# Seven products in the first stage's down part, and the attention mask added later

## The chip, the cores and the metric

One core of a Trainium2 chip runs the whole program. The metric is the device time of one execution in microseconds (us). The engines are TensorE (PE, matmuls into eight PSUM banks), VectorE (DVE), ScalarE (ACT), GpSimd (POOL) and SyncE (SP, which issues the weight loads). They run side by side and wait for each other through semaphores only.

## The reference

Input is x, 256 tokens of 1024 values in float32. A first block and two layers of a second block are computed, ten steps with a residual in all. The first step and the second, which this case is about, are:

```
f = (silu(n @ w_gate) * (n @ w_up)) @ w_down      # n = rms_norm(h) * pre gain; 1024 -> 2816 -> 1024
h = h + 0.5 * rms_norm(f) * post gain
q, k, v, xp, g_attn, g_pool = split(rms_norm(h) @ w_in)
s = q k^T / 8 over a neighbourhood + rpb bias; softmax; @ v    # 8 heads
m = (sigmoid(g_attn) * (y @ w_br_attn) + sigmoid(g_pool) * (pool(xp) @ w_br_pool)) @ w_out
h = h + rms_norm(m) * post gain
```

Then follow a second feed-forward step, a gated step on p, and the second block (feed-forward, gated linear attention, feed-forward, twice, the second time with retention). Everything is held to float32 accuracy.

## The kernel before

**Precision.** TensorE multiplies a reduced float32 format (fp32r). Each weight tile and each stationary block of tokens is therefore split in two: a high part, which ACT makes by a copy into fp32r (L1554 for weights), and a low part, the rest, which DVE makes by a subtraction (L2029). A product takes three runs of matmuls: high x high, token low x weight high (both want the high part), token high x weight low (wants the low part, so that comes last). A weight tile is 4 x 128 rows by 512 columns (1 MB, four "k"); the head tiles of the down weights have two k.

**Passes and products.** `pe_pass` multiplies one weight tile with one of two halves t of the tokens: 3 x 4 = 12 matmuls of 128x512, so a tile costs 24 (12 for a head tile). `pe_product` is one product of Strassen's scheme in Winograd's form: four tiles (two by two) with two token halves take seven products of 12 matmuls in place of eight passes of 12. It needs sums of token blocks (made and split once) and sums of weight tiles: t1 and t3 are a loaded tile to which POOL adds another by an accumulating DMA (`pool_sum`, L704), t2 and t4 are sums that DVE makes (L2033). The names of the products are b11, t1, t2, b22, t3, b21, t4.

**Stages.** The six feed-forward stages are f1, f2, a0, a1, b0, b1. Their gate and up part is an order of steps ("tile", "product", "turn"). A turn transposes 256 of the 2816 hidden values of both token halves (PE, L842), ACT copies it into `th` (L1559) and DVE makes `tl` (L2076). The last turns ("closing") lie in the down part. The down part has six row groups: group 0 (two k) and groups 1 to 5 (four k); group g needs the turned pieces 2g-1 and 2g. In f2, a0, a1, b0 and b1 the groups 2 and 3 are done as a unit of seven products (`pe_unit`, `dve_unit`, `DOWN_UNIT`); f1 does all groups in passes, group after group, with turns 8 and 7 behind groups 0 and 1. In all stages groups 4 and 5 close: first the four tiles for token half 0, then for token half 1, and ahead of the last pass PE transposes the next stage's x of token half 0 (`pe_turn_x`). The next stage starts with three passes and then transposes token half 1.

**The unit.** For it ACT copies four turned pieces once more, into `ua`, which lies in the buffer of the gains (L1700, ahead of the copy into `th`); DVE makes four sums `us`, ACT and DVE split them into `ush` and `usl`, which lie in the buffers `xh` and `xl` of the stage's x. In f2, whose result needs an rms norm before it goes into h, the products' shares are gathered in `xn` (`act_shared`, L1789; `take`, L2392), and at the edge DVE adds xn and the PSUM bank (L2116) before the arithmetic below. In a0 to b1 they are added to h directly.

**The edge** (`act_edge`, `dve_edge`; `to_mix` behind f1). For each token half ACT squares and sums the result (L1613), DVE multiplies it with a gain (L2122), adds up (L2124), ACT takes the root, DVE inverts it and updates h (L2133) and x (L2099). Between these the first tiles of the next stage are split: `early`, `mid`, `late` of the edge, (2, 1, 1) tiles for `to_mix`, (1, 2, 1) for most others. `src` is a PSUM bank.

**Weights.** SP loads tile after tile in the order of `load_key` and waits before each until its block is free. In f1 twelve blocks (of 14) hold whole, high and low parts; a planner (`give_blocks`, `give_slots`) gives each tile the block whose last user is oldest, a slot being a fixed pair of blocks. Blocks 12 and 13 hold the attention bias. ACT and DVE split in tile order, as far ahead as the blocks allow (`ahead`, `behind`, `act_high`, `dve_lows`).

**POOL's order.** Gains 1 and 2 by DMA, the mask, 16 parts of the bias with the four additions of f1 between them, then 16 additions of the mask to the bias (L722, each behind a given low of DVE), then gains 3 and 4 (each behind the last use of the gain before it), then three constants of the mixer, issued behind f1's last pass. The mixer's DVE adds the bias to the scores (L2479, one call for each head of two and each of 8 units), after a wait for the bias of its two heads.

Of the kernel before, what the change touches and what calls it, by code (L numbers as in the profile page):

```python
# [59 lines left out]
UNIT_ROWS = (2, 3)  # L60
# [18 lines left out]
UNIT_IN = ("f2", "a0", "a1", "b0", "b1")  # L79
# [82 lines left out]
def build(nc, A, out):  # L162
    with ExitStack() as ctx:
# [35 lines left out]
        xh = sb("xh", [P, 8, 256], F32R)  # L199
        xl = sb("xl", [P, 8, 256], F32R)  # L200
# [177 lines left out]
        def plan_ffn(name):  # L378
# [20 lines left out]
            if name not in UNIT_IN:  # L399
                plan_rows(name + "d", A[f"w_{name}_down"], A[f"w_{name}_down_head"])  # L400
                return
# [5 lines left out]

            p, q = UNIT_ROWS
            for step, *what in DOWN_UNIT:
# [55 lines left out]
        to_mix = edge(0, "mix", "rms", (1, 2), 4.0, "f1d", (2, 1, 1))  # L465
# [48 lines left out]
        def give_ffn(name, among, into_mixer=False):  # L514
# [5 lines left out]
            if name in UNIT_IN:  # L520
# [172 lines left out]
        def pool_sums(pool, name):  # L693
            for g in [group[name, n] for n in range(len(ORDER[name].pairs))] + (
                    [group[name + "d", 0]] if name in UNIT_IN else []):
# [10 lines left out]
        def pool_program(pool):  # L706
# [4 lines left out]
            pool_gain(pool, 1)  # L711
            pool_gain(pool, 2)
# [40 lines left out]
            pool.dma_start(pw[:, :, :], A["pool_w"][0].rearrange("g c d -> c g d")).then_inc(mix_in.mark("all"), 16)  # L753

# [68 lines left out]
        def unit_part(name, j):  # L823

            return [(m, 2 * j + 2 - 4 * g) for m, g in enumerate(UNIT_ROWS)
                    if name in UNIT_IN and 4 * g - 2 <= 2 * j < 4 * g + 2]

# [194 lines left out]
        def pe_ffn(pe, f):  # L1022
# [72 lines left out]
            if name in UNIT_IN:  # L1095
                pe_unit(pe, f, turn)
                dn = [None] * 8 + [spot[name + "d", g, n] for g in (4, 5) for n in range(2)]
            for g in range(0 if name in UNIT_IN else 4):
# [11 lines left out]
            for t in range(2):  # L1110
                for n in range(4):
# [5 lines left out]
                    if (t, n) == (1, 3) and f.nx == "out":  # L1117
                        if name in UNIT_IN:
# [5 lines left out]
        def pe_unit(pe, f, turn):  # L1124
# [10 lines left out]
            def tile(g, n):  # L1135
                for t in range(2):
                    if g == 0 and n == 1:
                        pe.wait_ge(vec.sem, vec.of("mult", name, order.plain[-2], t))
                    if n == 0 and t == 0:
                        pe.wait_ge(turn_lo.sem, turn_lo.of("t", name, order.last_turned(2 * g)))  # L1140
                    pe_pass(pe, spot[name + "d", g, n], T, groups[g][0], t, ACC[t][n], g == 0, False)

            def product(m):
                if m == "b11":
                    pe.wait_ge(turn_lo.sem, turn_lo.of("t", name, max(range(3, 7), key=order.turned.index)))
                    pe_product(pe, grp.b11, *block(0, grp.first), bank[0], True)
                elif m == "t1":
                    pe.wait_ge(fn.sem, fn.of("ush", name))
                    pe.wait_ge(vec.sem, vec.of("usl", name))
                    pe_product(pe, grp.t1, *sums(0), bank[1], True)  # L1150
                elif m == "t2":
                    if name == "f2":
# [3 lines left out]
                    pe_product(pe, grp.t2, *sums(1), bank[0], False)  # L1156
                elif m == "b22":
                    pe_product(pe, grp.b22, *sums(3), ACC[0][1], False)
                elif m == "t3":
                    pe.wait_ge(vec.sem, vec.of("ud", name, 0, 1, "t2"))  # L1160
                    pe_product(pe, grp.t3, *sums(2), bank[0], False)
                elif m == "b21":
                    pe_product(pe, grp.b21, *block(0, grp.second), ACC[0][0], False)
                else:
                    pe_product(pe, grp.t4, *block(1, grp.second), ACC[1][0], False)

            for step, *what in DOWN_UNIT:
# [431 lines left out]
        def act_post(act, e, t):  # L1599
# [5 lines left out]
            src = [half(xn[:, t, :], j) for j in range(2)] if e.nx == "pg" else edge_source(e, t)  # L1605
            for j in range(2):
                if e.kind == "ple":
                    act.wait_ge(vec.sem, vec.of("em", j, t))
                elif e.nx == "pg":
# [65 lines left out]
        def act_ffn(act, f, e):  # L1675
# [19 lines left out]
            def turn(j):  # L1695
                for m, k in unit_part(name, j):
                    act.wait_ge(turned.sem, turned.of("t", name, j))
                    if j == min(range(3, 7), key=order.turned.index):
# [62 lines left out]
            if name in UNIT_IN:  # L1761
                for step, *what in DOWN_UNIT:
                    if step == "tile":
                        act_high(act, ahead(spot[(name + "d", *what)], 1))
                    elif step == "product":
                        act_high(act, ahead(spot[name + "d", 0, what[0]], 1))
                        if name == "f2" and what[0] in ("b11", "t1", "t3"):
# [3 lines left out]
                    elif step == "blocks":  # L1771
                        act.wait_ge(vec.sem, vec.of("us", name, 3))
                        act.wait_ge(passed.sem, passed.of(gu[-1], 1))
                        act.activation(ush[:, :, :, :], us[:, :, :, :], ACT.Copy).then_inc(fn.mark("ush", name), 1)
# [7 lines left out]
        def act_shared(act, name, m):  # L1782
            act.wait_ge(passed.sem, passed.of(spot[name + "d", 0, m], 1))
            if m == "b11":
                act.wait_ge(vec.sem, vec.of("usl", name))
            if m == "t3":
                act.wait_ge(vec.sem, vec.of("ud", name, 1, 1, m))
            for t, n, b in {"b11": ((0, 0, 0),), "t1": ((0, 1, 1), (1, 1, 1)), "t3": ((1, 0, 0),)}[m]:
                act.activation(half(xn[:, t, :], n), bank[b][:, :], ACT.Copy).then_inc(fn.mark("ud", name, m), 1)  # L1789
# [500 lines left out]
        def dve_ffn(dve, f, e):  # L2290
# [76 lines left out]
            if name in UNIT_IN:  # L2367
# [8 lines left out]
        def dve_unit(dve, f, e, turn):  # L2376
# [11 lines left out]
            def take(t, n, after, m):  # L2388
# [3 lines left out]
                dve.tensor_tensor(x, x, bank[0][:, :], ALU.subtract).then_inc(vec.mark("ud", name, t, n, m), 1)  # L2392

            def products(m):
                if name == "f2":
# [4 lines left out]
                elif m == "b11":  # L2400
                    add(0, 0, bank[0], 1.0, m)
                elif m == "t1":
                    add(0, 1, bank[1], 1.0, m)
                    add(1, 1, bank[1], 1.0, m)
                elif m == "t2":
                    add(0, 1, bank[0], -1.0, m)
                elif m == "t3":
                    add(1, 1, bank[0], -1.0, m)
                    add(1, 0, bank[0], 1.0, m)
# [458 lines left out]
```

## Time and profile before

| | us |
|---|---|
| median of three runs | 1577.14 (1576.97 to 1578.09) |
| the profiled execution | 1576.5 |
| its span, first to last instruction | 1574.7 |
| PE busy in the span | 1564.3 |
| DVE busy | 1225.4 |
| ACT busy | 919.2 |
| POOL busy | 116.9 |

The granted TensorE clock was 0.999 of full speed. The busy time of PE includes matmuls that overlap; what one costs is read from the starts of those behind each other. In a timeline row the numbers are the start, the duration, the engine, the line, the operation, the written and read tiles, and how many instructions of the kind lie together; in brackets the idle time before them and what ended it.

### The profile page before, as it was taken

To read this page: it belongs to the slowest core of one execution; us is meant where nothing else is said; L and a number is where in the kernel's file an instruction comes from. 1 tells how busy PE (TensorE), PEld (TensorE's weight loads), DVE (VectorE), ACT (ScalarE), POOL (GpSimd) and SP (SyncE) were. 2 spreads that over 40 slices of the span, in tenths; PEclk is the share of its full clock that TensorE was granted. 3 is DMA by queue.
4 is the path that set the end of the run, shared out by engine and by line. 5 is a ranking of instruction groups with operands and counts; after the bars stand their busy time and mean duration, and the time that the engine had idled before them with its cause. 6 is when DMAs were issued, how large, how long until landed. Compare 5 with 4: busy or idle time off the path is not lost.

```text
span 1574.7 us, 18788 instructions
## 1 busy us (share of the span) xinstructions
PE 1564.3 (99%) x7587; PEld 1303.4 (83%) x7587; DVE 1225.4 (78%) x1168; ACT 919.2 (58%) x957; POOL 116.9 (7%) x138
## 2 busy tenths in 40 slices
PE   9999999999999999999999999999999999999998
PEld 6878897788888888888988888888888998888886
DVE  6888466677889779888658898878897657688887
ACT  7556456656675776654655575466654435455752
POOL 1115000000000000001010000000000131000000
PEclk9999999999999999999999999999999999999999
DMA  9896464467876687674648777868775544576773
GB/s 347 263 272 240 161 237 144 147 244 225 273 247 233 236 285 256 213 242 181 241 161 293 211 244 218 325 209 290 241 267 206 191 170 149 194 279 210 255 219 134
DMA packets 54484, 360.25 MB, mean 229 GB/s; under 512 B 6528, under 2 KB 6912, under 8 KB 13696
## 3 DMA queue, kind: packets, MB, share of 16 engines
q1 hardware_dynamic: 44864, 308.24, 52.0%
q0 software_dynamic: 9312, 50.70, 14.5%
q8 instruction: 60, 0.98, 0.3%
q14 instruction: 24, 0.20, 0.0%
q10 hardware_dynamic: 224, 0.14, 0.0%
HBM read 358.00 MB, written 1.05 MB: 228 GB/s over the span
## 4 chain that ended last, share of the span: by engine, by line
PE 98%; DVE 1%; DMA 0%; issue 0%; ACT 0%; SPq 0%; DVEq 0%; ACTq 0%
PE bank L892 22%; PE bank L905 22%; PE bank L896 19%; PE bank L959 7%; PE bank L954 7%; PE bank L956 7%; PE bank L842 3%; PE bank L909 3%; PE bank L988 2%; PE bank L990 2%; PE bank L991 2%; DVE split L2029 0%; DMA whole<-in_w_f_gate_up 0%; PE bank L1436 0%; PE bank L1226 0%; DVE whole L2033 0%
## 5 line engine op out<-in xcount | busy, mean ns | idle before, releaser
L2029 DVE TENSOR_TENSOR split<-whole,split 128x2048 fp32r<-128x2048 f32 (+2 forms) x346 | 741.8, 2168 | 113.5 <-ACT split L1554 112.6
L1554 ACT ACTIVATE split<-whole 128x2048 fp32r<-128x2048 f32 (+1 forms) x331 | 615.6, 1879 | 235.1 <-DVE whole L2033 59.8
L892 PE MATMUL bank<-split,xh 128*128 128x512 f32 x1020 | 279.6, 396 | 0.0
L905 PE MATMUL bank<-split,xh 128*128 128x512 f32 x1020 | 273.6, 390 | 0.0
L896 PE MATMUL bank<-split,xl 128*128 128x512 f32 x848 | 227.2, 390 | 0.0
L905 PEld LDWEIGHTS bank<-split,xh 128*128 128x128 f32 x1020 | 191.1, 188 | 40.8 <-DVE split L2029 0.6
L892 PEld LDWEIGHTS bank<-split,xh 128*128 128x128 f32 x1020 | 186.8, 188 | 39.4 <-issue 3.0
L896 PEld LDWEIGHTS bank<-split,xl 128*128 128x128 f32 x848 | 159.2, 188 | 34.2
L892 PE MATMUL bank<-split,th 128*128 128x512 f32 x364 | 101.0, 394 | 0.0
L896 PE MATMUL bank<-split,tl 128*128 128x512 f32 x364 | 99.4, 389 | 0.0
L905 PE MATMUL bank<-split,th 128*128 128x512 f32 x364 | 99.4, 389 | 0.0
L896 PEld LDWEIGHTS bank<-split,tl 128*128 128x128 f32 x364 | 68.3, 188 | 14.4
L905 PEld LDWEIGHTS bank<-split,th 128*128 128x128 f32 x364 | 68.3, 188 | 14.4
L892 PEld LDWEIGHTS bank<-split,th 128*128 128x128 f32 x364 | 67.1, 188 | 13.0
L2033 DVE TENSOR_TENSOR whole<-whole 128x2048 f32<-128x2048 f32 x34 | 77.6, 2284 | 0.0
L988 PE MATMUL bank<-xh,split 128*128 128x256 f32 x256 | 72.6, 284 | 0.0
L990 PE MATMUL bank<-xl,split 128*128 128x256 f32 x256 | 72.4, 283 | 0.0
L991 PE MATMUL bank<-xh,split 128*128 128x256 f32 x256 | 72.4, 283 | 0.0
L954 PE MATMUL bank<-split,xh 128*128 128x512 f32 x224 | 61.4, 396 | 0.6 <-DVE xn L2303 0.6
L2076 DVE TENSOR_TENSOR tl<-bank,th 128x512 fp32r<-128x512 f32 x66 | 45.4, 687 | 20.8 <-ACT th L1559 20.2
L956 PE MATMUL bank<-split,xl 128*128 128x512 f32 x224 | 60.0, 390 | 0.0
L959 PE MATMUL bank<-split,xh 128*128 128x512 f32 x224 | 60.0, 390 | 0.0
(335 smaller groups left out, 1998.5 us busy)
## 6 DMA issues: line engine op xcount, KB each, us to landing
whole<-in_w_a_gate_up SPq DMA_DIRECT2D x48, 1024.0 KB, 6.9
whole<-in_w_b_gate_up SPq DMA_DIRECT2D x48, 1024.0 KB, 6.9
whole<-in_w_f_gate_up SPq DMA_DIRECT2D x46, 1024.0 KB, 8.2
whole<-in_w_ret SPq DMA_DIRECT2D x24, 1024.0 KB, 4.8
whole<-in_w_a_down SPq DMA_DIRECT2D x22, 1024.0 KB, 6.8
whole<-in_w_b_down SPq DMA_DIRECT2D x22, 1024.0 KB, 6.8
whole<-in_w_f_down SPq DMA_DIRECT2D x21, 1024.0 KB, 4.9
whole<-in_w_mix SPq DMA_DIRECT2D x16, 1024.0 KB, 4.9
```

What stands on the lines that cost most here:

```text
L892: pe.matmul(o[:, :], tokens(0, k), whi[:, k, :], start=start and k == 0, stop=False, skip_group_check=True)
L896: pe.matmul(o[:, :], tokens(1, k), whi[:, k, :], start=False, stop=False, skip_group_check=True)
L905: ins = pe.matmul(o[:, :], tokens(0, k), wlo[:, k, :], start=False, stop=end, skip_group_check=True)
L954: pe.matmul(o[:, :], xh_of(k), whi[:, k, :], start=start and k == 0, stop=False, skip_group_check=True)
L956: pe.matmul(o[:, :], xl_of(k), whi[:, k, :], start=False, stop=False, skip_group_check=True)
L959: ins = pe.matmul(o[:, :], xh_of(k), wlo[:, k, :], start=False, stop=k == 3, skip_group_check=True)
L988: pe.matmul(o, whi[:, k, cols], xh[:, k0 + k, :], start=start and k == 0 and c % 2 == 0, stop=False, skip_group_check=True)
L990: pe.matmul(o, whi[:, k, cols], xl[:, k0 + k, :], start=False, stop=False, skip_group_check=True)
L991: ins = pe.matmul(o, wlo[:, k, cols], xh[:, k0 + k, :], start=False, stop=end, skip_group_check=True)
L1554: act.activation(split[s][:, 0:n], whole[r][:, 0:n], ACT.Copy).then_inc(hi.mark(i), 1)
L2029: dve.tensor_tensor(split[r][:, c0:c1], whole[r][:, c0:c1], split[s][:, c0:c1].bitcast(F32), ALU.subtract).then_inc(lo.mark(*what), 1)
L2033: dve.tensor_tensor(whole[load_to[i]][:, :], whole[load_to[a]][:, :], whole[load_to[b]][:, :], ALU.add).then_inc(vec.mark("sum", i), 1)
```

## The change

f1 gets a unit too, of the row groups 1 and 2 (`UNIT["f1"]`), with its own orders for PE and ACT (`F1_UNIT`) and DVE (`F1_UNIT_DVE`): tiles of groups 0 and 3 and the turns 8 and 7 lie between the products. Turns 1 to 4 make the second copy into `ua`; since `ua` lies in the gains' buffer, gains 1 and 2 are loaded only after the sums (`pool_gain(pool, g, "f1")`), behind the unit's two additions by DMA. The sums lie in `usx`, on the memory of `xl`, since `xn` still holds products of gate and up; they wait for the last pass over x. The products' banks are 6 and 7. Like f2, f1 gathers the shares in `xn`, so its edge adds xn and the bank first. The edge's tiles are (1, 2, 1), and only the last four down tiles get fixed slots. The 16 mask additions move behind gains 3 and 4 and the mixer's constants, in an order by pairs of heads, and no longer wait for DVE's lows.

```diff
+F1_UNIT = (
+    ("tile", 0, 0), ("tile", 0, 1), ("blocks",), ("turn", 8), ("tile", 3, 0), ("turn", 7),
+    ("product", "b11"), ("tile", 3, 1), ("product", "t1"), ("product", "b22"),
+    ("product", "t2"), ("product", "b21"), ("product", "t3"), ("product", "t4"))
+F1_UNIT_DVE = (
+    ("sums",), ("lows", 0, "b11"), ("turn", 8), ("blocks",), ("turn", 7), ("lows", 3, 1), ("lows", 0, "t1"),
+    ("lows", 0, "b22"), ("lows", 0, "t2"), ("lows", 0, "b21"),
+    ("add", "t2"), ("lows", 0, "t3"), ("lows", 0, "t4"), ("add", "t3"))
...
+UNIT = {"f1": Unit((1, 2), F1_UNIT, F1_UNIT_DVE),
+        **{name: Unit((2, 3), DOWN_UNIT, DOWN_UNIT_DVE) for name in ("f2", "a0", "a1", "b0", "b1")}}
+GATHERED = {"f1": "mix", "f2": "pg"}
...
+        with ExitStack() as first:
+            usx = sb("usx", [P, 4, 4, P], F32, first)
         xl = sb("xl", [P, 8, 256], F32R)
...
-        to_mix = edge(0, "mix", "rms", (1, 2), 4.0, "f1d", (2, 1, 1))
+        to_mix = edge(0, "mix", "rms", (1, 2), 4.0, "f1d", (1, 2, 1))
...
-                    give_slots(end - 4, end, [[5], [6], range(5), range(5)])
+                    closing = [[s] for s in slots if s >= 5]
+                    give_slots(end - 4, end, closing + [range(5)] * (4 - len(closing)))
...
-            pool_gain(pool, 1)
-            pool_gain(pool, 2)
...
-            for t in range(2):
-                pool.wait_ge(bias_in[t].sem, bias_in[t].of(7))
-                for hd in range(8):
-                    pool.wait_ge(lo.sem, lo.of(at["f1d"][t] + hd // 2))
-                    pool_mask(t, hd)
+            pool_sum(pool, "t1", group["f1d", 0].t1)
+            pool_sum(pool, "t3", group["f1d", 0].t3)
+            for g in (1, 2):
+                pool_gain(pool, g, "f1")
             for g in (3, 4):
                 pool_gain(pool, g)
...
             pool.dma_start(pw[:, :, :], A["pool_w"][0].rearrange("g c d -> c g d")).then_inc(mix_in.mark("all"), 16)
+            for t in range(2):
+                pool.wait_ge(bias_in[t].sem, bias_in[t].of(7))
+            for n in range(16):
+                pool_mask(n // 2 % 2, 2 * (n // 4) + n % 2)
...
+                    if g == 0 and n == 0 and name == "f1":
+                        pe.wait_ge(vec.sem, vec.of("mult", name, order.plain[-1], t))
...
-            src = [half(xn[:, t, :], j) for j in range(2)] if e.nx == "pg" else edge_source(e, t)
+            src = [half(xn[:, t, :], j) for j in range(2)] if e.nx in GATHERED.values() else edge_source(e, t)
...
+                        i = ahead(spot[(name + "d", *what)], 1)
+                        act_high(act, min(i, group[name + "d", 0].b11) if what[0] == 0 else i)
...
-            if e.nx == "pg":
-                dve.wait_ge(fn.sem, fn.of("ud", "f2", "t3"))
+            if e.nx in GATHERED.values():
+                dve.wait_ge(fn.sem, fn.of("ud", "f1" if e.nx == "mix" else "f2", "t3"))
...
             def sums():
-                dve.wait_ge(turned.sem, turned.of("t", name, ORDER[name].turned[-2]))
-                dve.wait_ge(fn.sem, fn.of("ua", name, max(range(3, 7), key=ORDER[name].turned.index)))
+                us = unit_sums(name)
+                if name == "f1":
+                    dve.wait_ge(passed.sem, passed.of(at[name + "gu"][-1], 1))
+                else:
+                    dve.wait_ge(turned.sem, turned.of("t", name, ORDER[name].turned[-2]))
+                dve.wait_ge(fn.sem, fn.of("ua", name, unit_turned(name)[-1]))
```

## Rows read from the trace of the kernel before

**Rows 1.** The page's first part: busy us (share of the span), instructions.

```profile
PE 1564.3 (99%) x7587; PEld 1303.4 (83%) x7587; DVE 1225.4 (78%) x1168; ACT 919.2 (58%) x957; POOL 116.9 (7%) x138
```

**Rows 2.** Waits of PE: engine line, releaser: us in all, times, longest.

```profile
PE bank L959 <- DVE split L2029: 0.7, 1, 0.7
PE bank L954 <- DVE xn L2303: 0.6, 1, 0.6
```

**Rows 3.** Timeline of PE, down part: start us, us, engine, line.

```profile
130.32 0.61 PE L892 MATMUL bank<-split,th 128*128 128x512 f32 x2
...
163.93 1.07 PE L892 MATMUL bank<-split,th 128*128 128x512 f32 x4
164.83 1.07 PE L896 MATMUL bank<-split,tl 128*128 128x512 f32 x4
```

**Rows 4.** Timeline of ACT, second stage, a turn of the unit.

```profile
444.58 0.60 ACT L1700 ACTIVATE gain<-bank 128x512 f32<-128x512 f32 x1
445.06 0.60 ACT L1559 ACTIVATE th<-bank 128x512 fp32r<-128x512 f32 x1
```

**Rows 5.** Timelines of ACT, DVE and PE behind turn 3.

```profile
60.56 0.60 ACT L1559 ACTIVATE th<-bank 128x512 fp32r<-128x512 f32 x1 [3.53 <-PE bank L842]
...
61.19 0.69 DVE L2076 TENSOR_TENSOR tl<-bank,th 128x512 fp32r<-128x512 f32 x1 [1.83 <-ACT th L1559]
...
70.61 2.28 DVE L2029 TENSOR_TENSOR split<-whole,split 128x2048 fp32r<-128x2048 f32 x1
...
73.59 4.48 DVE L2029 TENSOR_TENSOR split<-whole,split 128x2048 fp32r<-128x2048 f32 x2
...
72.18 1.07 PE L956 MATMUL bank<-split,sl 128*128 128x512 f32 x4
...
75.93 1.20 PE L905 MATMUL bank<-split,xh 128*128 128x512 f32 x4
```

**Rows 6.** Timeline of DVE, down part: a low beside masks.

```profile
142.83 2.84 DVE L2029 TENSOR_TENSOR split<-whole,split 128x2048 fp32r<-128x2048 f32 x1 [0.59 <-ACT split L1554]
```

**Rows 7.** Weight tiles, 130 to 200 us, and timeline of ACT, second stage.

```profile
DMA to landing us min/median/max: 4.7/4.9/7.0
...
502.30 1.92 ACT L1554 ACTIVATE split<-whole 128x2048 fp32r<-128x2048 f32 x1 [0.59 <-DMA whole<-in_w_f_down]
504.87 1.92 ACT L1554 ACTIVATE split<-whole 128x2048 fp32r<-128x2048 f32 x1 [0.65 <-DMA whole<-in_w_f_down]
```

**Rows 8.** Timelines of ACT, DVE and PE, edge into the mixer.

```profile
192.25 1.92 ACT L1554 ACTIVATE split<-whole 128x2048 fp32r<-128x2048 f32 x1 [2.12 <-DMA whole<-in_w_mix]
...
194.20 2.29 DVE L2029 TENSOR_TENSOR split<-whole,split 128x2048 fp32r<-128x2048 f32 x1 [3.24 <-ACT split L1554]
196.41 1.28 DVE L2122 TENSOR_TENSOR xn<-bank,gain 128x512 f32<-128x512 f32 x2
197.61 0.15 DVE L2124 TENSOR_TENSOR st<-st 128x1 f32<-128x1 f32 x1
...
199.30 1.07 PE L905 MATMUL bank<-split,xh 128*128 128x512 f32 x4
200.39 1.26 PE L842 MATMUL bank<-ident,xn 128*128 128x128 f32 x8
```

**Rows 9.** Timelines of DVE and ACT, closing arithmetic of the second stage.

```profile
514.23 0.69 DVE L2116 TENSOR_TENSOR xn<-xn,bank 128x512 f32<-128x512 f32 x1 [1.23 <-PE bank L905]
...
514.96 0.63 ACT L1613 ACTIVATE junk<-xn 128x512 bf16<-128x512 f32 x1 [1.20 <-DVE xn L2116]
...
515.71 0.69 DVE L2122 TENSOR_TENSOR xn<-xn,gain 128x512 f32<-128x512 f32 x1 [0.19 <-ACT junk L1613]
```

**Rows 10.** Mask additions (min/median/max ns), timelines of POOL and DVE.

```profile
L722 POOL TENSOR_TENSOR bias<-bias,mask x16: 731/745/2834, 128.2 to 148.3; 128x256 f32<-128x256 f32 x16
...
202.84 0.77 POOL L753 DMA_DIRECT2D pw<-in_pool_w  x1
...
243.30 0.74 DVE L2479 TENSOR_TENSOR pr<-bank,bias 128x256 f32<-128x256 f32 x2
```

More of the change, by code:

```diff
@@ L406, in rows @@
                 return full[g - 1, n] if g else head[n]
-            p, q = UNIT_ROWS
-            for step, *what in DOWN_UNIT:
+            p, q = UNIT[name].rows
+            for step, *what in UNIT[name].steps:
                 if step == "tile":
@@ L823, in unit_part, with unit_turned, unit_bank, unit_sums @@
         def unit_part(name, j):
-            return [(m, 2 * j + 2 - 4 * g) for m, g in enumerate(UNIT_ROWS)
-                    if name in UNIT_IN and 4 * g - 2 <= 2 * j < 4 * g + 2]
+            return [(m, 2 * j + 2 - 4 * g) for m, g in enumerate(UNIT[name].rows) if 4 * g - 2 <= 2 * j < 4 * g + 2]
+        def unit_turned(name):
+            p, q = UNIT[name].rows
+            return sorted([j for g in (p, q) for j in (2 * g - 1, 2 * g)], key=ORDER[name].turned.index)
+        def unit_bank(name, n):
+            return bank[6 + n] if name == "f1" else bank[n]
+        def unit_sums(name):
+            return (usx if name == "f1" else us)[:, :, :, :]
         def turn_bank(pe, key, by):
@@ L1155, in product @@
                         pe.wait_ge(vec.sem, vec.of("ud", name, 0, 0, "b11"))
-                    pe_product(pe, grp.t2, *sums(1), bank[0], False)
+                    pe_product(pe, grp.t2, *sums(1), unit_bank(name, 0), False)
                 elif m == "b22":
-                    pe_product(pe, grp.b22, *sums(3), ACC[0][1], False)
+                    pe_product(pe, grp.b22, *sums(3), acc[0][1], False)
                 elif m == "t3":
                     pe.wait_ge(vec.sem, vec.of("ud", name, 0, 1, "t2"))
-                    pe_product(pe, grp.t3, *sums(2), bank[0], False)
+                    pe_product(pe, grp.t3, *sums(2), unit_bank(name, 0), False)
                 elif m == "b21":
-                    pe_product(pe, grp.b21, *block(0, grp.second), ACC[0][0], False)
+                    pe_product(pe, grp.b21, *block(0, grp.second), acc[0][0], False)
                 else:
-                    pe_product(pe, grp.t4, *block(1, grp.second), ACC[1][0], False)
-            for step, *what in DOWN_UNIT:
+                    pe_product(pe, grp.t4, *block(1, grp.second), acc[1][0], False)
+            for step, *what in UNIT[name].steps:
                 if step == "tile":
@@ L1697, in turn @@
                     act.wait_ge(turned.sem, turned.of("t", name, j))
-                    if j == min(range(3, 7), key=order.turned.index):
+                    if j == unit_turned(name)[0] and name != "f1":
                         act.wait_ge(vec.sem, vec.of(*gain_end[e.gains[0] - 1]))
@@ L1773, in act_ffn @@
                         act.wait_ge(passed.sem, passed.of(gu[-1], 1))
-                        act.activation(ush[:, :, :, :], us[:, :, :, :], ACT.Copy).then_inc(fn.mark("ush", name), 1)
+                        act.activation(ush[:, :, :, :], unit_sums(name), ACT.Copy).then_inc(fn.mark("ush", name), 1)
             else:
@@ L1788, in act_shared @@
             for t, n, b in {"b11": ((0, 0, 0),), "t1": ((0, 1, 1), (1, 1, 1)), "t3": ((1, 0, 0),)}[m]:
-                act.activation(half(xn[:, t, :], n), bank[b][:, :], ACT.Copy).then_inc(fn.mark("ud", name, m), 1)
+                act.activation(half(xn[:, t, :], n), unit_bank(name, b)[:, :], ACT.Copy).then_inc(
+                    fn.mark("ud", name, m), 1)
         def act_mixer(act):
@@ L2425, in dve_unit @@
             added = {}
-            for step, *what in DOWN_UNIT_DVE:
+            for step, *what in UNIT[name].dve:
                 if step == "sums":
```

60 lines of the change are left out of this document (30 added, 30 removed).

## The prediction

> **What bounds the kernel now.** I read the page's busy times first, then TensorE's waits, then the timelines of PE, DVE, ACT and POOL from 28 to 262 us (first feed-forward stage and head of the mixer), and last the second feed-forward stage, which already has such a unit. TensorE is busy 1564.3 of 1574.7 us [rows 1]: it is the bound, and time is won by taking matmuls out or lost by making it wait. Two of its four listed waits are in the first stage, both short and both ended by DVE: 0.65 us for a product of gate and up, 0.74 us for the low half of a weight tile [rows 2]. So DVE is the engine to fear there.
>
> All instants below are on the clock of the trace of before; the unit lies at 130.3 to 166.7 us, and what follows it moves 2.72 us earlier if nothing waits.
>
> **The matmuls.** Row groups 1 and 2 of the down weights took eight passes of 12 matmuls, 96; the seven products take 84. Groups 0, 3, 4 and 5 keep theirs, and the two transpositions stay. Four matmuls start every 0.90 to 0.91 us (163.93, 164.83) [rows 3], 0.227 us each, not the 0.39 a row shows for one, since they overlap. Gain: 12 x 0.227 = 2.72 us, all on the path. It is also all that the change can give by its own terms.
>
> **The four copies into ua (ScalarE, gate and up phase).** Turns 1 to 4 now copy the transposed block a second time, ahead of the copy into th. In the second stage the second copy starts 0.48 us after the first (444.58, 445.06) [rows 4]. At turns 1, 2 and 4 the delay falls into idle time of ACT or DVE (turn 2: DVE then idles 1.8 us; turn 4: DVE is in a row of lows until 82.4). Turn 3 is different. th starts at 60.56, DVE's tl at 61.19, right behind it, and from there DVE works without a gap to 82 us. The low half of t2 ran 70.61 to 72.89, and PE wants it at 72.18 + 0.91 = 73.09; the low of tile (9,0) starts at 73.59, ends at 75.87, and PE takes it at 75.93, 0.06 later: it is already just in time [rows 5]. With 0.48 more, t2's low is there at 73.43 (0.34 lost) and the next at 76.41 for 75.93. Loss 0.48 us. Bounds: 0 (if DVE starts its row earlier), and 4 x 0.48 = 1.9.
>
> **DVE and ACT inside the unit.** Added: four sums, one split of them (ush, usl), two weight sums, three more weight splits on each engine, some copies and takes. A low or a weight sum costs DVE 2.20 us (two in 4.48) [rows 5]. By the new order and its planner's rule DVE reaches the four sums at about 132 (gate/up ends at 130.3; [rows 3]), earlier than the last multiplication's 134.8 of before since tile (3,0) is left for the unit. From 132.2: sums 2.6, (3,0) 2.2, b11 2.2, tl(8) 0.7, usl 2.2 (142.1); tl(7) waits for its turn to 143.5; (3,1) 2.2, sum 2.2, t1 2.2 (150.1), b22 2.2, sum 2.2, t2 2.2 (156.7), b21 158.9, take, t3 162.0, t4 164.2. PE wants the lows two thirds into each product: t1 152.1, b22 154.8, t2 157.5, b21 160.2, t3 162.9, t4 165.7. The least slack is 0.8 us, so 0 taken. Bounds: 0, and 1.7 us (if DVE reaches the sums at 134.8 as its old work did: 2.6 less 0.9). The 16 mask additions leave this stretch, where they stretched lows (one to 2.84 from 2.28) [rows 6]; that helps DVE and is worth nothing, as PE did not wait.
>
> **The closing weights.** I followed the planner's oldest-block rule. The four closing tiles A to D need slots that the products just used, and slot 6 is closed in this stage. A and B are freed by t1, b22 and b21 and come early; C's block is freed only by t3, at 163.9, and D, and the mixer's tiles 0 and 1, queue behind it on SP. A load lands 4.9 us after its issue (median; 4.7 to 7.0), and loads in a row come 2.5 us apart (502.30, 504.87) [rows 7]. C: 169.0, high 171.0, low 173.3; PE needs 172.1 and 173.9. D: 171.5, low 175.8, needed 176.6. Slack 0.6: 0 taken. Upper bound with the 7.0 us landing: low at 175.4, 1.5 us lost. Tile 0 of the mixer then comes at 174.0, later than now, its low ends at 178.3, the two additions at 179.6, and the rest of token half 0's arithmetic takes as long as now, some 5 us; PE wants its result at 185.7, so about 1 us of slack is left there.
>
> **The edge into the mixer.** This is the second loss. For token half 1 everything hangs on the mixer's tile 2, whose block is freed by a closing pass: it arrives at 192.2, ACT splits it, DVE makes its low (194.20 to 196.4), then the products with the gain start (196.41), their sum of squares at 197.61, and PE's transposition of the normed x, which could have begun at 199.30 + 0.91 = 200.21 starts at 200.39: this chain has no slack at all now [rows 8]. The change puts the addition of xn and the bank ahead of it: y0 and y1 (0.60 each, behind one another), and the square can only start behind y. In the second stage y1 starts at 514.23, its square at 514.96, the gain product at 515.71 [rows 9]: 1.48 from y1's start to the second gain product. So with the low ended at 196.41: y1 at 197.01, second gain product 198.5, the small sum at 199.16 in place of 197.61. Loss 1.55 us. Both the load and PE move by the same 2.72, so the difference stands. Bounds: 0, and 3.0 (four extra instructions of 0.69 and a handoff, all in line).
> The order (1,2,1) of the edge's loads takes one low from before token half 0's arithmetic to behind it; DVE has 1 to 2 us there: nothing.
>
> **Gains and masks.** Gains 1 and 2 are now loaded behind the unit's sums and t3's addition, at about 142, more than 30 us before the closing arithmetic wants the first: nothing. POOL's queue then has gains 3 and 4, three constants, and the masks. The last constant is issued at 202.84; a mask takes 0.745 us (median) and 2.834 at the longest; the first logit, at 243.30, needs four masks [rows 10]. Even at 2.834 each the first four are done by 214.2 and all sixteen by 248.2, when no more than the third logit is due, which needs eight: nothing. The other side of it is DVE: the mask's extra 2.1 us and the 0.56 us that a low grew to 2.84 show that the two hold each other up, and four or five lows of the mixer's head will now lie beside masks. That is the third rival. The Trainium skill (SBUF — State Buffer, "Who interferes with whom") has it as a rule: a DVE instruction with two SBUF inputs and a GpSimd one that reads SBUF exclude each other for a whole instruction; the trace agrees in kind, and by the rule a low could wait for a whole mask, 0.745 us, rather than 0.56.
>
> **Sum.** -2.72 + 0.48 + 1.55 = -0.69 us. The profiled execution took 1576.5 (span 1574.7 and 1.8 around it), 0.6 under the median 1577.14 of the three timed runs: 1576.5 - 0.7 = 1575.8, and against the median 1577.1 - 0.7 = **1576.4**.
>
> **Rivals.**
> 1. Everything is hidden: 1577.1 - 2.7 = 1574.4. For: the same unit in the second stage runs without a PE wait, and its y additions too. Against: there the closing chain does not hang on a load freed by the last passes. Between it and mine (one of the two losses only): 1574.9 or 1576.0.
> 2. The other side: C comes late. Its load hangs on t3's pass, 8.2 us before its first use and 10.0 before PE wants its low, where landing, high and low take 4.9 + 1.9 + 2.3 = 9.1, with handoffs 9.4. From a landing of over 5.5 us PE waits one for one; over 6.2 the kernel is slower than before. At 7.0: -0.69 + 1.5 = +0.8, so 1577.9; if D and the unit's lows slip as well (+1.7), 1579.6. For: the 7.0 occurs in this stretch [rows 7], and no other stage has a closing slot less. Against: 4.9 is usual.
> 3. The masks lengthen five lows of DVE in the mixer's head by 0.56 each, and PE waits for all of it: +2.8, 1579.2. Against: DVE idles between these lows, waiting for ACT, and they end well ahead of PE.
> That the products would not replace the passes I rule out by the code.
>
> **Chances.** Mine 0.50, rival 1 (with its halves) 0.25, rival 2 0.17, rival 3 0.03, something unseen 0.05. A difference under 0.2% (3.2 us) can't be told from none here. Even rival 1 stays inside, so faster 0.05 (an unseen wait that goes), slower 0.08 (the deep end of rival 2, rival 3), same 0.87. Range: from 1574.2, just under rival 1, to 1578.8, inside rival 2.
>
> **What would show it.** Right: 12 fewer 128x512 matmuls on th/tl and blocks (252 in the stage, 84 of them products); near 73 us a PE wait on DVE grown by 0.3 and the tile behind by 0.1; the unit free of waits; PE waiting some 1.7 us for the transposition near 198 to 199 us, with DVE's addition, ACT's square and the gain product in line before it. Wrong: a PE wait on ACT or DVE for a weight tile in the closing passes (rival 2), no wait at the transposition (rival 1), the logits waiting for POOL. If mixer tile 2 arrives earlier relative to PE, my largest loss falls.

## The result and the profile after

The changed kernel takes 1589.83 us (median of 6 runs, 1589.11 to 1591.33), the one before beside it 1577.17 (6 runs): ratio 1.0081, 95% interval 1.0069 to 1.0093. It is 12.7 us slower where I forecast 0.7 faster, far outside my range. The profiled execution took 1589.11 us, its span is 1587.1 at a mean granted clock of 0.996.

The page's busy row and TensorE's waits of the changed kernel (line, releaser: us in all, times, longest):

```profile
PE 1565.6 (99%) x7575; PEld 1303.0 (82%) x7575; DVE 1253.8 (79%) x1184; ACT 930.5 (59%) x969; POOL 109.4 (7%) x140
...
PE bank L917 <- ACT xh L1586: 11.0, 1, 11.0
PE bank L984 <- DVE split L2060: 0.9, 2, 0.8
PE bank L979 <- DVE xn L2334: 0.6, 1, 0.6
```

The 12 matmuls are gone (7587 to 7575 against [rows 1]), the waits of [rows 2] are about as they were, and one wait is new and nearly as large as the whole loss. Its releaser reads "ACT xh", the copy of the mixer's normed x; but ACT had been idle itself, so the chain has to be followed one step further. The timeline of DVE, PE, POOL and ACT around it (start, duration, engine, line; in brackets the idle time before it and its releaser):

```profile
198.90 1.26 PE L867 MATMUL bank<-ident,xn 128*128 128x128 f32 x8 [0.34 <-DVE xn L2130]
...
199.36 2.36 DVE L2060 TENSOR_TENSOR split<-whole,split 128x1024 fp32r<-128x1024 f32 x2
...
201.31 0.77 POOL L763 DMA_DIRECT2D pw<-in_pool_w  x1
...
201.63 11.41 DVE L2135 TENSOR_TENSOR st<-st 128x1 f32<-128x1 f32 x1
201.84 1.07 PE L930 MATMUL bank<-split,xh 128*128 128x512 f32 x4
202.09 10.93 POOL L733 TENSOR_TENSOR bias<-bias,mask 128x256 f32<-128x256 f32 x16
213.08 0.29 ACT L1617 ACTIVATE st<-st,eps 128x1 f32<-128x1 f32 x1 [13.46 <-DVE st L2135]
213.28 1.06 ACT L1586 ACTIVATE xh<-bank 128x512 fp32r<-128x512 f32 x2
213.41 0.16 DVE L2138 RECIPROCAL st<-st 128x1 f32<-128x1 f32 x1 [0.36 <-ACT st L1617]
...
213.91 2.08 PE L917 MATMUL bank<-split,xh 128*128 128x512 f32 x4 [11.00 <-ACT xh L1586]
...
215.78 1.91 PE L930 MATMUL bank<-split,xh 128*128 128x512 f32 x4
...
218.81 1.07 PE L917 MATMUL bank<-split,xh 128*128 128x512 f32 x4
```

Read from the bottom: PE waits for ACT's copy, ACT for its root, the root for DVE's small sum of squares, one element per partition. That sum is recorded with 11.41 us, and in just that time GpSimd runs all sixteen mask additions without a break. By the recorded starts the sum even comes first, 0.46 us ahead of the first mask. In the kernel before, the same sum and the low ahead of it:

```profile
200.85 2.36 DVE L2029 TENSOR_TENSOR split<-whole,split 128x1024 fp32r<-128x1024 f32 x2
203.13 0.16 DVE L2104 TENSOR_TENSOR st<-st 128x1 f32<-128x1 f32 x1
```

The second part of the loss stands in the windows of the changed kernel (the stretch, its length, then the busy us of PE, PE's weight loads, DVE, ACT and POOL, then the granted clock, DMA share, GB/s):

```profile
199.00:202.00 3.00, 3.00 (x17) 2.47 (x18) 3.00 (x4) 0.62 (x3) 2.26 (x4) 1.00 0.39 132
202.00:213.90 11.90, 0.91 (x5) 0.41 (x3) 11.54 (x6) 0.82 (x3) 11.01 (x17) 0.76 0.38 129
213.90:218.80 4.90, 4.89 (x12) 3.85 (x13) 2.75 (x4) 3.40 (x4) 0.00 (x0) 0.55 0.00 0
218.80:222.00 3.20, 3.20 (x16) 2.64 (x15) 0.82 (x1) 0.27 (x1) 0.00 (x0) 1.00 0.58 177
```

After 11 us of idling the granted clock is 0.55, near the lower level of 1.2 GHz, and 12 matmuls take 4.90 us where twelve at full clock take 2.72: 2.18 us more. Then it is back at 1.00.

The sum from the first stage to the second feed-forward stage: 0.45 (the gate and up phase starts that much later in this execution) + 0.48 (turn 3) - 2.72 (matmuls) + 0.32 (transposition) + 11.16 (from the last matmul's end at 202.75 to 213.91) + 2.18 (clock) = 11.87. The two traces are 11.82 apart there (479.00 against 467.18 for the same matmul). The spans differ by 12.4; the other 0.6 come later, most of it (0.36) behind the end of b0, where e12 below takes it up.

### The profile page after: what moved, and what is told of

Its sections match the earlier page's. It is cut to its first block, busy times and chain, and to the rows that moved or that the text cites. A ratio compares the mean times of both kernels' runs of the same rounds, so it can differ in the third digit from the quotient of the medians.

```text
span 1587.1 us, 18811 instructions
## 1 busy us (share of the span) xinstructions
PE 1565.6 (99%) x7575; PEld 1303.0 (82%) x7575; DVE 1253.8 (79%) x1184; ACT 930.5 (59%) x969; POOL 109.4 (7%) x140
## 4 chain that ended last, share of the span: by engine, by line
PE 93%; DVE 3%; DMA 1%; ACT 1%; issue 1%; SPq 0%; DVEq 0%; ACTq 0%
PE bank L917 21%; PE bank L930 20%; PE bank L921 17%; PE bank L984 7%; PE bank L979 7%; PE bank L981 7%; PE bank L867 3%; PE bank L934 3%; PE bank L1013 2%; PE bank L1015 2%; PE bank L1016 2%; DVE split L2060 1%; DVE st L2135 1%; DMA whole<-in_w_mix 1%; DVE whole L2064 1%
## 5 line engine op out<-in xcount | busy, mean ns | idle before, releaser
L917 PE MATMUL bank<-split,xh 128*128 128x512 f32 x1020 | 280.7, 397 | 11.0 <-ACT xh L1586 11.0
L930 PE MATMUL bank<-split,xh 128*128 128x512 f32 x1020 | 274.4, 391 | 0.0
L917 PEld LDWEIGHTS bank<-split,xh 128*128 128x128 f32 x1020 | 187.3, 189 | 51.0 <-ACT xh L1586 11.4
L921 PE MATMUL bank<-split,xl 128*128 128x512 f32 x848 | 227.2, 390 | 0.0
L917 PE MATMUL bank<-split,th 128*128 128x512 f32 x332 | 92.3, 394 | 0.0
L930 PE MATMUL bank<-split,th 128*128 128x512 f32 x332 | 90.9, 390 | 0.1
L921 PE MATMUL bank<-split,tl 128*128 128x512 f32 x332 | 90.8, 390 | 0.0
L2064 DVE TENSOR_TENSOR whole<-whole 128x2048 f32<-128x2048 f32 x36 | 82.2, 2284 | 0.0
L930 PEld LDWEIGHTS bank<-split,th 128*128 128x128 f32 x332 | 62.2, 188 | 13.6 <-DVE split L2060 0.5
L921 PEld LDWEIGHTS bank<-split,tl 128*128 128x128 f32 x332 | 62.3, 188 | 13.2
L917 PEld LDWEIGHTS bank<-split,th 128*128 128x128 f32 x332 | 61.1, 188 | 11.8
L979 PE MATMUL bank<-split,xh 128*128 128x512 f32 x240 | 65.7, 395 | 0.6 <-DVE xn L2334 0.6
L981 PE MATMUL bank<-split,xl 128*128 128x512 f32 x240 | 64.3, 390 | 0.0
L984 PE MATMUL bank<-split,xh 128*128 128x512 f32 x240 | 64.3, 390 | 0.0
```

The costliest lines, as they stand in the source:

```text
L917: pe.matmul(o[:, :], tokens(0, k), whi[:, k, :], start=start and k == 0, stop=False, skip_group_check=True)
L921: pe.matmul(o[:, :], tokens(1, k), whi[:, k, :], start=False, stop=False, skip_group_check=True)
L930: ins = pe.matmul(o[:, :], tokens(0, k), wlo[:, k, :], start=False, stop=end, skip_group_check=True)
L979: pe.matmul(o[:, :], xh_of(k), whi[:, k, :], start=start and k == 0, stop=False, skip_group_check=True)
L981: pe.matmul(o[:, :], xl_of(k), whi[:, k, :], start=False, stop=False, skip_group_check=True)
L984: ins = pe.matmul(o[:, :], xh_of(k), wlo[:, k, :], start=False, stop=k == 3, skip_group_check=True)
```

## The experiments

**Theory A:** a burst of GpSimd additions with no wait between them keeps a two-input instruction of DVE out until the burst ends, however small that instruction is. **Rivals:** the loss comes from the unit or from the edge's new additions; or a mere overlap with masks costs it, whatever their spacing.

**e1_gap.** Each mask first waits for the mark of the one before it on its own engine:

```
             for n in range(16):
+                if n:
+                    pool.wait_ge(gp.sem, gp.of("bias", (n - 1) // 2 % 2, 2 * ((n - 1) // 4) + (n - 1) % 2))
                 pool_mask(n // 2 % 2, 2 * (n // 4) + n % 2)
```

> The changed kernel, with one wait more: each mask addition on POOL first waits for the end of the one before. Theory A (sixteen additions issued without a wait between them keep DVE's two-input instruction out until the last is done, 11.4 us in the trace; a wait in between lets it in): the small DVE sum at the mixer's head takes under 2 us, PE's 11.0 us wait and the 2.2 us of slow matmuls behind it go, the span falls by about 13 us, to 1574, and the time to some 1576. Theory B (whatever the waits, DVE is kept out as long as POOL has additions to do): no change, 1589 to 1590. Theory C (the 11 us belong to the DMA issues of gains and constants ahead of the additions, not to the additions): no change either.

Measured: 1578.41 us, ratio to before 1.0011 (1.0003 to 1.0020). DVE and POOL of its timeline:

```profile
202.67 1.24 DVE L2137 TENSOR_TENSOR st<-st 128x1 f32<-128x1 f32 x1
203.13 19.97 POOL L733 TENSOR_TENSOR bias<-bias,mask 128x256 f32<-128x256 f32 x15
...
204.78 1.20 PE L919 MATMUL bank<-split,xh 128*128 128x512 f32 x4 [0.82 <-ACT xh L1588]
...
208.21 2.76 DVE L2062 TENSOR_TENSOR split<-whole,split 128x2048 fp32r<-128x2048 f32 x1 [2.05 <-ACT split L1583]
```

The same sixteen masks at the same place, each now followed by a short gap, and the time falls by 11.4 us. That is theory A; the time is 2.4 us above the 1576 that I expected. The sum still loses 1.1 us, to one mask; the low beside them grows to 2.76, as in [rows 6].

**e2_old_place.** The masks back in the stage, each behind its low, ahead of t3's sum (and gone from behind the constants):

```
             pool_sum(pool, "t1", group["f1d", 0].t1)
+            for t in range(2):
+                pool.wait_ge(bias_in[t].sem, bias_in[t].of(7))
+                for hd in range(8):
+                    pool.wait_ge(lo.sem, lo.of(at["f1d"][t] + hd // 2))
+                    pool_mask(t, hd)
             pool_sum(pool, "t3", group["f1d", 0].t3)
```

> The changed kernel with the sixteen mask additions back where they were, each pair behind a low of DVE in the down part, between the unit's two additions by DMA; so the unit alone, with the late gains. Theory A: no wait of 11 us; the three terms of the prediction as the trace has them now, -2.72 for the matmuls, +0.48 for turn 3, +0.3 for the transposition at the edge, give 1575.2 against 1577.2 of before. But t3's addition by DMA starts behind the masks, near 150 us, and PE wants its high part at 162: up to 2 us may be lost there. Theory C: 11 us stay.

Measured: 1594.89 us, ratio 1.0114 (1.0100 to 1.0128): slower still. POOL's and PE's timelines:

```profile
137.71 26.81 POOL L733 TENSOR_TENSOR bias<-bias,mask 128x256 f32<-128x256 f32 x12 [4.76 <-DVE split L2061]
164.47 0.87 POOL L717 DMA_DIRECT2D whole<-in_w_f_down  x1
...
161.25 1.24 PE L985 MATMUL bank<-split,xh 128*128 128x512 f32 x4 [2.35 <-DVE split L2061]
178.00 2.08 PE L980 MATMUL bank<-split,xh 128*128 128x512 f32 x4 [11.22 <-DVE xn L2424]
```

A miss of mine. With the unit in it DVE is busy 24.76 of these 26.76 us (in the kernel before 26.95 of the down part's 39.05), and the twelve masks take turns with its instructions: a mask takes 2.75 us (median) instead of 0.71. t3's DMA addition is queued behind them on POOL, is issued at 164.47 only, and PE waits 11.2 us for what follows. So the masks can't stay ahead of t3's sum. The old place with t3's sum ahead of the masks was not tried; that they must leave the stage is therefore not shown.

**e3_masks_alone.** The kernel before, with the move of the masks and nothing else:

```
-                for hd in range(8):
-                    pool.wait_ge(lo.sem, lo.of(at["f1d"][t] + hd // 2))
-                    pool_mask(t, hd)
...
+            for t in range(2):
+                pool.wait_ge(bias_in[t].sem, bias_in[t].of(7))
+            for n in range(16):
+                pool_mask(n // 2 % 2, 2 * (n // 4) + n % 2)
```

> The kernel before, with nothing but the sixteen mask additions moved behind gains 3 and 4 and the constants, without waits between them; no unit in the first stage. Theory A: the whole loss is here, 11.2 + 2.2 = 13.4 us over before, some 1590.5, with a DVE instruction of about 11 us. Rival (the loss needs the unit, for instance the later chain of the edge or the gathering in xn): 1577, no such instruction.

Measured: 1590.97 us, ratio 1.0087 (1.0073 to 1.0101).

```profile
203.62 11.44 DVE L2103 TENSOR_TENSOR st<-st 128x1 f32<-128x1 f32 x1
204.10 10.94 POOL L722 TENSOR_TENSOR bias<-bias,mask 128x256 f32<-128x256 f32 x16
...
215.93 2.08 PE L891 MATMUL bank<-split,xh 128*128 128x512 f32 x4 [10.71 <-ACT xh L1558]
```

The whole loss (13.6 us over the 1577.41 of before beside it), without unit or edge: those rivals are out.

**e4_burst_later.** The burst stays, but its first mask waits for DVE's xl, behind the small sum: `+ pool.wait_ge(turn_lo.sem, turn_lo.of("x", "mix", 1, 1))` ahead of the loop.

> The changed kernel, with one wait before the first mask addition, for the last low half of the mixer's x; then all sixteen without waits between. Theory A: the small sum is spared, and the next DVE instruction with two inputs from SBUF, the low of the mixer's fifth weight tile, is kept out instead, about 8 us. PE wants that low some 8 us after the burst starts, so the loss shrinks to 0 to 4 us: 1575 to 1579. Rival B2 (only a tiny DVE instruction starves, a 128x2048 low alternates with the additions as it did before, 2.3 to 2.9 us): the low takes under 3 us and the time is 1575 to 1576.

Measured: 1577.47 us, ratio 1.0002 (0.9993 to 1.0011).

```profile
202.94 0.15 DVE L2136 TENSOR_TENSOR st<-st 128x1 f32<-128x1 f32 x1
...
205.40 13.22 POOL L733 TENSOR_TENSOR bias<-bias,mask 128x256 f32<-128x256 f32 x16 [2.02 <-DVE xl L2108]
...
207.38 2.30 DVE L2061 TENSOR_TENSOR split<-whole,split 128x2048 fp32r<-128x2048 f32 x1 [2.16 <-ACT split L1582]
214.91 5.86 DVE L2061 TENSOR_TENSOR split<-whole,split 128x2048 fp32r<-128x2048 f32 x1 [5.23 <-ACT split L1582]
```

One wait, placed where nothing hangs on it, takes the loss away. The two lows qualify theory A: the first got in between two masks and one mask took 2.78 us instead; the second took 5.86 us and ended some 2 us after the burst (218.6), so it was kept out for some 3.7 us. So large instructions are kept out as well, but not each time; what decides at a mask's boundary is open.

**e5_bursts_of_4 and e6_bursts_of_8.** e1's wait only ahead of every fourth (`if n and n % 4 == 0:`), or every eighth mask (`n % 8`).

> The changed kernel, with a wait for the end of the previous addition before every fourth mask addition, so bursts of four. So far: with no wait DVE's small sum lasts until the 16th addition is done (11.4 us), with a wait before each it lasts 1.2 us. If the length of the burst sets it, it now lasts four additions, 4 x 0.70 + 0.45 = 3.2 us, and PE waits some 3 us at the mixer's head: about 3 us more than the version with a wait before each would need without its waits, 1578 to 1581. If any single gap were as good as sixteen or as bad as none: 1.2 or 11.4 us.

> The same with one wait, before the ninth addition: the small sum lasts eight additions, 8 x 0.70 + 0.45 = 6.0 us, PE waits 5.8 us, and where its clock falls behind the wait another 1 to 2 us go: 1581 to 1585. If the burst's length did not matter: as bursts of four, or as the changed kernel.

Measured: e5 1581.22 us, ratio 1.0022 (1.0013 to 1.0032); e6 1585.45, ratio 1.0050 (1.0036 to 1.0063). The small sum of e5, then that of e6:

```profile
203.00 3.27 DVE L2137 TENSOR_TENSOR st<-st 128x1 f32<-128x1 f32 x1
```

```profile
203.64 5.97 DVE L2137 TENSOR_TENSOR st<-st 128x1 f32<-128x1 f32 x1
...
210.19 0.97 DVE L2482 TENSOR_SCALAR xn<-ident,st 128x128 f32<-128x128 f32 x2
...
210.47 2.07 PE L919 MATMUL bank<-split,xh 128*128 128x512 f32 x4 [5.54 <-ACT xh L1588]
```

Bursts of 1, 4, 8 and 16 give 1.24, 3.27, 5.97 and 11.41 us: 0.56 + 0.68 for each mask of the burst fits all four within 0.03, and the masks of the changed kernel's burst start 0.68 apart (10.93 for sixteen). This is the price, by length. Both times lie just above what I expected: the clock costs more than I allowed. Behind PE's wait of 2.86 us twelve matmuls took 4.44 us (207.13 to 211.57) in e5, behind 5.54 us 5.29 (210.47 to 215.76) in e6, where 2.72 is the full clock; behind 0.82 us in e1 the granted clock stayed at 1.00. The pair of TENSOR_SCALAR instructions above takes 0.97 us in both runs instead of 0.35. In e6 it lies in the second burst of eight, so DVE's instruction with one tensor input lost about one mask there, not the burst.

**e7_late_and_gap.** e4's late start and e1's gaps together.

> The changed kernel with both repairs: the first mask addition waits for the last low half of the mixer's x, and each further one for the end of the one before. Theory A: neither the small sum nor any low is kept out for more than one addition, so PE waits nowhere for it; what is left is the unit: -2.7 for the matmuls, +0.5 for turn 3, +0.4 for the transposition at the edge: 1575.6 against 1577.4 of before. If it comes out at 1577 to 1578 like the two half repairs, then something else of the change costs the 2 us.

Measured: 1577.46 us, ratio 1.0000 (0.9991 to 1.0008). The small sum takes 0.16, the first lows beside masks 2.54 and 2.57, and PE waits for none of them. The interference is gone, but the time is the 1577 to 1578 that I had set for "something else costs the 2 us".

**e9_sum_ahead.** e7, and in the edge the two additions of y for token half 1 go ahead of the low of the mixer's tile 2:

```
-                for j in range(2):
+                for j in range(0 if (e.nx, t) != ("mix", 1) else 2, 2):
...
+            if e.nx == "mix":
+                dve.wait_ge(fn.sem, fn.of("ud", "f1", "t3"))
+                for j in range(2):
+                    x = half(xn[:, 1, :], j)
+                    dve.wait_ge(passed.sem, passed.of(e.final[2 + j], 1))
+                    dve.tensor_tensor(x, x, edge_source(e, 1)[j], ALU.add).then_inc(vec.mark("y", e.nx, 1, j), 1)
```

> As the version with both repairs, and at the edge into the mixer DVE adds xn and the bank for token half 1 ahead of the low of the mixer's third weight tile instead of behind it, so that ACT's squares run beside that low. The gain products then start right behind the low and the small sum comes 1.3 us earlier; PE's wait at the transposition (0.34 us in the changed kernel) goes. Gain against the version with both repairs: 0.3 to 0.4 us, which only the profile can show. If the chain hung on something else, the wait stays.

Measured: 1576.94 us, ratio 0.9998 (0.9989 to 1.0006). The wait at the transposition (0.34 us in the changed kernel, 0.42 in e7) is gone, and no other takes its place at the edge. From turn 0's transposition (the first in the gate and up part, 31.27 us in before) to the transposition at the end of b0 (1190.52 in before) it needs 1157.28 us against 1159.25, yet its time is before's. Where the 2 us went was open; three more runs took that up, and the question whether the number of masks or their size keeps DVE out.

**e11_short_masks.** The changed kernel with each mask cut to one element per partition (`bias[:, t, hd, 0, 0:1]`, `mask[:, 0:1]`).

> The kernel after with the sixteen mask additions cut to one element per partition each (of 256), at the same place and still without a wait between them: the mask is left out of the rest of the bias. Theory A (DVE's two-input instruction is kept out as long as GpSimd's additions follow each other): what counts is how long the burst lasts, so with additions of some 0.1 to 0.2 us the small sum takes 0.45 us plus the whole burst at most, 2 to 3.5 us, not 11.4, and the time is 1577 to 1580. Rival (the price is per instruction of GpSimd, whatever its size): the small sum takes near 11 us again and the time stays at 1589. A second rival, that instructions this short leave DVE room between them: the small sum takes under 0.6 us, no wait of TensorE at the edge beyond 0.4, and 1576.5 to 1577.5.

Measured: 1577.18 us, ratio 0.9997 (0.9988 to 1.0006).

```profile
203.08 0.16 DVE L2135 TENSOR_TENSOR st<-st 128x1 f32<-128x1 f32 x1
...
203.54 2.37 POOL L733 TENSOR_TENSOR bias<-bias,mask 128x1 f32<-128x1 f32 x16
```

The time stays at before's, so sixteen additions in a row are not enough by their number. But theory A had 2 to 3.5 us here, and the sum lost nothing, as in the second rival. The sum starts 0.46 us ahead of the first mask, as it does in the changed kernel (201.63 against 202.09), where it was held all the same; so the records don't show how long masks get hold of it before their recorded start (spans on POOL are rough). As the sum was never caught here, the run doesn't tell what a burst of short additions would do to an instruction inside it. The dose above is for masks of 128x256.

**e10_before_again and e12_sum_ahead_again.** A second execution profiled of each.

> The kernel before once more, for a second profile of it. The repaired versions gain 1.4 to 2.0 us between turn 0's first product and the transposition at the end of b0 (1157.3 to 1157.9 us against 1159.25 in the first profile of before), but all their medians lie within 0.1% of before's. Theory S: the change itself costs in the head of the kernel. Then turn 0 of before starts again near 31.3 us, as in its first profile. Theory N: where turn 0 starts, 31.3 to 33 us, differs from execution to execution whatever the kernel. Then before may start it at 32 us or later too, and the stretch from there to the end of b0 stays at 1159.2 us within 0.5. Time 1577.2.

> The best version once more, on the same chip as the second profile of before: masks behind the edge with a gap before each, the additions of y's second token half ahead of the lows. If its gain of 1.97 us between turn 0 and the end of b0 stands and the head and tail are only scatter (theory N), the median is 0.5 to 1.8 us under before's; if the change costs in the head (theory S), it equals before's within 0.3 us, as the first time (ratio 0.9998), and turn 0 starts a microsecond or more later than in before's second profile.

Measured: e10 1577.6 us, ratio 1.0002 (0.9993 to 1.0011); e12 1576.62, ratio 0.9994 (0.9985 to 1.0003). Turn 0 and the far end in e10, then in e12:

```profile
32.11 0.60 PE L842 MATMUL bank<-ident,hh 128*128 128x128 f32 x4
...
1190.89 1.03 PE L842 MATMUL bank<-ident,h 128*128 128x128 f32 x8
```

```profile
32.57 0.60 PE L870 MATMUL bank<-ident,hh 128*128 128x128 f32 x4
...
1189.99 1.03 PE L870 MATMUL bank<-ident,h 128*128 128x128 f32 x8
```

The stretch takes 1158.78 and 1157.42: the gain is there in both pairs, 1.36 us in this one and 1.97 in the first. The head, up to turn 0, is 0.46 us longer in e12, and the tail, from the end of b0 on, is 0.40 longer (spans 1575.1 and 1574.6: 0.46 - 1.36 + 0.40 = -0.50). The thirteen profiles together say which of the two is scatter:

| | three without the unit (before, e10, e3) | ten with it |
|---|---|---|
| head: start of turn 0 | 31.27 to 32.51 | 31.73 to 32.97 |
| tail: end of b0 to the end of the span | 384.15 to 384.21 | 384.54 to 385.02 |

The heads overlap, so no cost of the change is shown there (theory N). In all thirteen turn 0 comes 22.25 to 22.50 us after PE's transposition of the second part of x (8.77 to 10.67), which in eleven of them waits for x's DMA: the scatter lies in these first microseconds. The tails don't overlap: every kernel with the unit is 0.3 to 0.9 us longer there. That is a cost of the change, and it takes back a part of the gain. The last weight tile, e10 first, then e12:

```profile
1535.45 8.49 SPq L650 DMA_DIRECT2D whole<-in_w_b_down  x4
...
1550.75 1.92 ACT L1554 ACTIVATE split<-whole 128x2048 fp32r<-128x2048 f32 x1 [0.56 <-DMA whole<-in_w_b_down]
```

```profile
1534.56 8.49 SPq L663 DMA_DIRECT2D whole<-in_w_b_down  x4
...
1551.00 1.93 ACT L1584 ACTIVATE split<-whole 128x2048 fp32r<-128x2048 f32 x1 [0.53 <-DMA whole<-in_w_b_down]
...
1552.85 1.20 PE L933 MATMUL bank<-split,th 128*128 128x512 f32 x4 [0.15 <-DVE split L2063]
```

The loads are issued 0.89 us earlier and the last tile is split 0.25 us later, waiting for its landing; PE waits a little. In e9 it is 1551.23. PE being ahead of its loads is not the reason: the changed kernel comes there 12 us later than before and its tail is 384.54 all the same, while e3, as late but without the unit, has 384.15. Why the last tiles come later in a kernel with the unit is open. e12's median is 0.80 us under before's, which is what theory N expected, but the interval of the ratio contains 1: no gain in time is shown.

## Why the prediction was wrong

**Gains and masks, "nothing": the step that failed.** I had the moved instructions counted, POOL's queue and the logits' due times right (the masks end at 213.0, the first logit doesn't wait for POOL), and I looked at DVE only for lows, at 0.56 each. What I didn't ask: the masks lose the waits on lows that stood ahead of each group, so they run as a burst, and which DVE instruction with two inputs lies in its first microsecond. It was the smallest one, 0.16 us, with ACT's root, the copies and PE's next product hanging on it and hardly any slack: in e1 it lost 1.08 us and PE waited 0.82. e3 shows the whole loss from this move alone, e1 and e4 that a gap or a later start removes it, e5 and e6 that it grows with the burst. Rival 3 named the pair of engines but its price was wrong by its unit: 0.56 per low taken from masks that alternate with lows [rows 6], where a burst costs its whole length once: 11.16, and 2.18 for the clock, instead of 2.8. The rule that I cited from the Trainium skill (SBUF — State Buffer, "Who interferes with whom") has exclusion for a whole instruction; e1's 1.24 us agrees with one mask, the 11.41 is sixteen of them, and that is not in the bound I drew from it. Which of the two engines goes first at a mask's boundary the records leave open: the sum was held in the changed kernel, a low got in at once in e4. My upper end should have been a burst.

**The matmuls, -2.72: right.** The unit runs from 131.25 to the first closing pass at 167.58, 36.33 us; in before the same stretch is 130.32 to 169.37, 39.05.

**Turn 3, +0.48: right.** Less the 0.45 by which this execution starts later, t2's low comes 0.34 late and the next tile's pass 0.48 (75.93 in [rows 5]), as forecast:

```profile
73.88 1.19 PE L984 MATMUL bank<-split,sh 128*128 128x512 f32 x4 [0.17 <-DVE split L2060]
...
76.86 1.19 PE L930 MATMUL bank<-split,xh 128*128 128x512 f32 x4
```

Putting the copy into ua behind that into th, to save it, was not tried.

**The unit, 0, and the closing weights, 0 (rival 2): right.** No wait of PE lies in either. ACT takes tile C, in the changed kernel, at

```profile
169.98 1.92 ACT L1581 ACTIVATE split<-whole 128x2048 fp32r<-128x2048 f32 x1 [3.41 <-DMA whole<-in_w_f_down]
```

which on the clock of before (0.93 less) is 169.05; I had 169.0. Rival 2 did not occur.

**The edge, +1.55: right in kind, too large.** The additions stand in line as I wrote:

```profile
189.07 1.92 ACT L1581 ACTIVATE split<-whole 128x2048 fp32r<-128x2048 f32 x1 [0.33 <-DMA whole<-in_w_mix]
191.22 2.28 DVE L2060 TENSOR_TENSOR split<-whole,split 128x2048 fp32r<-128x2048 f32 x1
193.42 1.28 DVE L2147 TENSOR_TENSOR xn<-xn,bank 128x512 f32<-128x512 f32 x2
194.89 1.31 DVE L2153 TENSOR_TENSOR xn<-xn,gain 128x512 f32<-128x512 f32 x2 [0.19 <-ACT junk L1640]
196.11 0.15 DVE L2155 TENSOR_TENSOR st<-st 128x1 f32<-128x1 f32 x1
```

From the low's start to the small sum 4.89 us against 3.41 in [rows 8]: 1.48 longer, where I had 1.55. But tile 2 landed 5.0 us after its issue instead of 6.3, so that its low started 1.17 us earlier against PE, and the loss was 0.32. I had named this as what would shrink it, and had no number for it.

Without the burst the sum would be 0.48 + 0.32 - 2.72 = -1.9. In the stretch from turn 0 to the end of b0 e4, e7 and e9 show -1.4 to -2.0 against the first profile of before and -0.9 to -1.5 against e10. The longer tail, 0.3 to 0.9 us, was in no term of my sum. None of their times can be told from before's.

## What to carry to other kernels

When elementwise work moves to GpSimd, or between its places there, count not only its time but its spacing: look for the DVE instruction with two inputs that will start in the burst, however tiny, and ask who hangs on it. A wait on an event that comes behind the critical instruction, or on the engine's own last result, breaks the burst for almost nothing. A wait that seems superfluous in the old code may be what kept the engines alternating (no run took only those waits away at the old place). And bound an interference by the longest run of the other engine's instructions, not by what one of them added in a place where they took turns.

## What the runs showed of the hardware that I had not expected

- A DVE addition of 128x1 took 1.24, 3.27, 5.97 and 11.41 us beside GpSimd bursts of 1, 4, 8 and 16 additions of 128x256, and 0.16 just ahead of sixteen of 128x1.
- The other way round, a GpSimd addition of 0.71 us took 2.75 us (median) in e2, where DVE was busy 93% of the time, and up to 2.87 (e5).
- Two DVE TENSOR_SCALAR of 128x128, which have one tensor input, took 0.97 us instead of 0.35 inside bursts of 4 and 8 (e5, e6): they lost about one mask, not the burst.
- An idle stretch of 11 us brought TensorE's granted clock to 0.55 over the next 4.9 us and cost 2.2 us on top. A stretch of 2.86 us did much the same (e5: 0.55 over the next 3.3 us, 1.7 us on top), one of 5.54 cost 2.6 (e6), and one of 0.82 left the clock at 1.00 (e1).
